# Routed outputs kept in DRAM until the last turn: stores and gathers in place of scatter matmuls

## What is computed

```python
ff = moe_swiglu(h, router_w[j], router_b[j], moe_w_gate[j], moe_w_up[j], moe_w_down[j])
x = x + g2 * ff
```

## Time and profile before

| What | Value |
|---|---|
| Median of 3 runs | 2793.11 us |
| Lowest and highest run | 2789.71 and 2797.35 us |
| The profiled execution | 2798.93 us |
| Its span, first to last instruction | 2797.2 us |
| Mean granted clock of TensorE | 0.992 |
| Busy, TensorE / VectorE / ScalarE / GpSimd | 2730.0 / 2003.7 / 1674.6 / 34.0 us |
| Read from and written to HBM | 695.19 and 8.91 MB |

### The profile page before, as it was taken

One profiled execution on the slowest core, in us unless ns is written; L12 is line 12 of the kernel. 1 busy time (PEld: TensorE's weight loads), 2 busy tenths in 40 slices (PEclk: granted clock), 3 DMA queues, 4 the chain that ended last, 5 costly groups with the idle time before them and its releaser, 6 DMA issues. The chain is left out here.

```text
span 2797.2 us, 39251 instructions
## 1 busy us (share of the span) xinstructions
PE 2730.0 (98%) x15544; PEld 2306.2 (82%) x15544; DVE 2003.7 (72%) x2123; ACT 1674.6 (60%) x1983; POOL 34.0 (1%) x60
## 2 busy tenths in 40 slices
PE   7999999999999999999999999999999999999998
PEld 5888999788978888888888888888868898867897
DVE  3766645586779989999898998986565556474555
ACT  3575544568457777777777777775354445353544
POOL 0000000000010000000000000001000000000000
PEclk8999999999999999999999999999999999999999
DMA  9847653765589999999999999975423453514451
GB/s 339 299 151 256 252 194 135 269 230 189 167 293 373 360 372 365 373 363 363 371 365 371 364 368 362 366 268 183 150 99 137 175 207 134 180 61 151 172 197 76
DMA packets 314443, 706.04 MB, mean 252 GB/s; under 512 B 7622, under 2 KB 26548, under 8 KB 314308
## 3 DMA queue, kind: packets, MB, share of 16 engines
q1 hardware_dynamic: 310336, 693.79, 69.0%
q0 software_dynamic: 3360, 10.16, 1.1%
q10 hardware_dynamic: 612, 0.18, 0.0%
HBM read 695.19 MB, written 8.91 MB: 252 GB/s over the span
## 5 line engine op out<-in xcount | busy, mean ns | idle before, releaser
L2731 DVE TENSOR_TENSOR ring_rest<-ring,weights_hi 128x2048 fp32r<-128x2048 f32 x270 | 608.3, 2283 | 10.1 <-ACT weights_hi L2056 8.1
L2056 ACT ACTIVATE weights_hi<-ring 128x2048 fp32r<-128x2048 f32 x270 | 516.6, 1915 | 134.7 <-PE ps L1782 71.6
L1780 PE MATMUL ps<-weights_hi,xg_hi 128*128 128x512 f32 x1008 | 402.4, 399 | 1.2 <-ACT arena L2056 0.6
L1782 PE MATMUL ps<-weights_hi,xg_lo 128*128 128x512 f32 x1008 | 395.1, 392 | 0.0
L1781 PE MATMUL ps<-ring_rest,xg_hi 128*128 128x512 f32 x792 | 309.9, 391 | 0.0
L2056 ACT ACTIVATE arena<-ps 128x512 f32<-128x512 f32 (+6 forms) x307 | 157.5, 529 | 220.5 <-PE ps L1782 54.1
L1801 PE MATMUL ps<-weights_hi,hidden_split_moe 128*128 128x512 f32 x1008 | 283.6, 393 | 0.1
L2731 DVE TENSOR_TENSOR ring_rest<-ring,mix_hi 128x2048 fp32r<-128x2048 f32 (+2 forms) x76 | 171.0, 2254 | 128.9 <-ACT mix_hi L2056 128.2
L2731 DVE TENSOR_TENSOR w_split<-ring,w_split 128x1024 fp32r<-128x1024 f32 x128 | 150.8, 1221 | 151.3 <-ACT w_split L2056 151.3
L2731 DVE TENSOR_TENSOR late_rest<-arena,weights_hi 128x2048 fp32r<-128x2048 f32 x108 | 245.3, 2285 | 5.5 <-ACT weights_hi L2056 4.5
L2056 ACT ACTIVATE weights_hi<-arena 128x2048 fp32r<-128x2048 f32 x108 | 207.1, 1918 | 65.9 <-PE ps L1782 36.0
(11 more groups left out here) (313 smaller groups left out, 5332.3 us busy)
## 6 DMA issues: line engine op xcount, KB each, us to landing
ring<-in_moe_w_gate_dram SPq DMA_DIRECT2D x54, 2048.0 KB, 8.5
ring<-in_moe_w_up_dram SPq DMA_DIRECT2D x45, 2048.0 KB, 9.2
ring<-in_moe_w_down_dram SPq DMA_DIRECT2D x36, 2048.0 KB, 8.2
ring<-in_mlp_w_dram SPq DMA_DIRECT2D x32, 2048.0 KB, 8.6
arena<-in_moe_w_down_dram SPq DMA_DIRECT2D x27, 2048.0 KB, 8.0
ring<-in_w_mod_dram SPq DMA_DIRECT2D x48, 1024.0 KB, 9.1
ring<-in_w_in_dram SPq DMA_DIRECT2D x48, 1024.0 KB, 6.1
arena<-in_moe_w_up_dram SPq DMA_DIRECT2D x18, 2048.0 KB, 8.0
```

The lines of the kernel that those rows point to most:

```text
L1780: pe.matmul(b, xg_hi[:, k, :], hi[:, i, :], start=(k == 0), stop=False)
L1782: mm = pe.matmul(b, xg_lo[:, k, :], hi[:, i, :], start=False, stop=(k == KD - 1))
L2056: return act.activation(o, i, func, **kw)
L2731: return dve.tensor_tensor(o, a, b, op)
```

## The change

A second DRAM table `y_rows` of the same shape as `slot_rows` is also filled with zeros, by eleven more writes. The event "scatter" goes, with its matmuls, its banks, its adds into x, and the rounding and splitting of the outputs in all turns but the last. In each turn but the first, SP stores `y_slots` (the outputs of the turn before) to that turn's 128 rows of `y_rows`, before the load of the twelfth of the 21 weights; SP has then waited for the first down product of this turn. VectorE waits for that store before it writes `y_slots` again. The first turn doesn't gate outputs that don't exist. When all turns are over (skipped ones count themselves), POOL gathers the rows of `y_rows` by `row_index` into `xn_moe`: two plain indirect DMAs for the first index of each token, a wait for them, and two accumulating ones for the second. VectorE adds the two tiles (128 x 1024) to x ahead of the last scatter, which stays. `weighted` moves to the place of `y_hi`, since `y_slots` now lives longer.

```diff
@@ expert_events, Tiles.expert_part
-        if what == "up" and half and g < 2:
-            events.append(("scatter", g))
-            elif kind == "scatter":
-                for t in range(TT):
-                    self.add(("scatter", e, at[0], t), "dve")
@@ program
-        slot_rows = nc.dram_tensor("slot_rows", (TURNS * P, D), F32).ap()
+        slot_rows, y_rows = (nc.dram_tensor(name, (TURNS * P, D), F32).ap() for name in ("slot_rows", "y_rows"))
+
+        def rows_of_turn(table, e):
+            return table.rearrange("(e p) d -> e p d", p=P)[bass.ds(e, 1)].rearrange("e p d -> p (e d)")
-        weighted = Region(y_at, TT * P).cut(TT, P)
         y_hi_at = expert.pos
+        weighted = Region(y_hi_at, TT * P).cut(TT, P)
@@ sync, load_turn; at its end in skipped turns, and once before the first turn
+                        if i == RING_B + expert_slots().index(("down", 0)):
+                            sp.dma_start(rows_of_turn(y_rows, turn - 1), y_slots).then_inc(sem("y_stored"), 16)
...
+                sp.sem_inc(sem("y_stored"), 16)
+
+            sp.sem_inc(sem("y_stored"), 16)
@@ gpsimd
                     for e in range(TURNS):
                         load(slot_rows[e * P:(e + 1) * P, :], blank, "slot_rows_blank")
+                        load(y_rows[e * P:(e + 1) * P, :], blank, "slot_rows_blank")
...
+            pool.wait_ge(sem("y_stored"), 16 * TURNS)
+            for n in range(2 * TT):
+                if n == TT:
+                    pool.wait_ge(sem("y_back"), 16 * TT)
+                pool.indirect_dma_start(xn_moe[:, n % TT], None, y_rows,
+                                        bass.IndirectOffsetOnAxis(row_index[:, n:n + 1], 0),
+                                        compute_op=ALU.bypass if n < TT else ALU.add).then_inc(sem("y_back"), 16)
 
             pool.wait_ge(pe_done, value["moe_down", TURNS - 1, GROUPS - 1])
             load(mem_nat, I["mem_2"][0].rearrange("(t p) d -> p t d", p=P), "mem_landed")
@@ tensor, expert_part
-                    elif kind == "scatter":
-                        c = at[0]
-                        if c == 0:
-                            pe.wait_ge(sem("to_tokens_hot_ready"), 1 + e)
-                        pe.wait_ge(sem("y_split_ready"), (c + 1) + e * 2)
-                        for t in range(TT):
-                            scatter(open_at(lambda i: ("scatter", i, c, t), e), t, c, y_hi[:, :])
@@ scalar, expert_head and expert_turn
-                    elif kind == "scatter":
-                        if at[0] == 0:
-                            act.wait_ge(pe_done, step_at(lambda i: ("scatter", i, 0, TT - 1), e))
-                            round_y(1, y_hi[:, :], e)
-                round_y(0, y_hi[:, :], e)
@@ vector
-            def first_half_of_y(e):
-
-                rest_of_y(0, y_hi[:, :], e)
+            def outputs_taken(e):
+
+                dve.wait_ge(sem("y_gated"), 2 * e)
                 dve.sem_inc(acc_emptied, 1)
...
-                        if (what, g, half) == ("gate", 1, 0):
-                            rest_of_y(1, y_hi[:, :], e)
-                    elif kind == "scatter":
-                        c = at[0]
-                        for t in range(TT):
-                            dve.wait_ge(pe_done, step_at(lambda n: ("scatter", n, c, t), e))
-                            xs = x[:, t, c * 512:(c + 1) * 512]
-                            tt(xs, xs, bank(("scatter", 0, c, t)), ALU.add).then_inc(emptied["dve"], 1)
@@ vector, expert_turn
+                dve.wait_ge(sem("y_stored"), e * 16)
                 gated_y(step_at(lambda i: ("moe_down", i, GROUPS - 1), e, 1))
                 rest_of_weights_of(4, e)
-                first_half_of_y(e)
+                outputs_taken(e)
@@ vector, first turn
+            dve.sem_inc(acc_emptied, 1)
             rest_of_routing()
-            gated_y(step_at(lambda i: ("moe_down", i, GROUPS - 1), 0, 1))
             rest_of_weights_of(4, 0)
-            first_half_of_y(0)
@@ vector, behind the last turn
+            def add_stored():
+
+                dve.wait_ge(sem("y_back"), 16 * 2 * TT)
+                for t in range(TT):
+                    tt(x[:, t], x[:, t], xn_moe[:, t], ALU.add).then_inc(sem("y_added"), 1)
+
+            dve.wait_ge(sem("y_stored"), 16 * TURNS)
             gated_y(value["moe_down", TURNS - 1, GROUPS - 1])
             for c in range(2):
-                rest_of_y(c, last_y_hi[:, c], TURNS)
+                rest_of_y(c, last_y_hi[:, c])
             dve.sem_inc(acc_emptied, 1)
+            add_stored()
+            dve.wait_ge(sem("y_added"), TT)
             for t in range(TT):
                 for c in range(2):
                     b = full(dve, ("last_scatter", 2 * t + c))
```

More of the change, by code:

```diff
@@ L735, in program @@
         expert.cut(HI_BUFFERS * 2048 + HALF_LINE)
-        y_hi, y_lo = rounded("y_hi", y_hi_at, 512), rounded("y_lo", y_at, 2, 512)
+        y_lo = rounded("y_lo", y_at, 2, 512)
         last_y_hi = rounded("last_y_hi", route_at, 2, 512)
@@ L1114, in load_turn @@
                             sp.wait_ge(sem("rows_scattered"), 16 * 2 * TT)
-                            rows_of_turn = slot_rows.rearrange("(e p) d -> e p d", p=P)[bass.ds(turn, 1)]
-                            sp.dma_start(rows_moe, rows_of_turn.rearrange("e p d -> p (e d)"))\
+                            sp.dma_start(rows_moe, rows_of_turn(slot_rows, turn))\
                                 .then_inc(sem("slot_rows_landed"), 16)
+                        if i == RING_B + expert_slots().index(("down", 0)):
+                            sp.dma_start(rows_of_turn(y_rows, turn - 1), y_slots).then_inc(sem("y_stored"), 16)
                     elif stream.before[n]:
@@ L1200, in _ @@
                                pattern=[[1, P]], channel_multiplier=-1).then_inc(sem("route_constants"), 1)
-            pool.wait_ge(sem("slot_rows_blank"), 16 * TURNS)
+            pool.wait_ge(sem("slot_rows_blank"), 32 * TURNS)
             pool.wait_ge(sem("row_index_ready"), 1)
@@ L1869, in _ @@
                 if i < 2:
-                    pe.wait_ge(sem("y_split_ready"), 2 * TURNS + i + 1)
+                    pe.wait_ge(sem("y_split_ready"), i + 1)
                 scatter(open_bank(("last_scatter", i)), i // 2, i % 2, last_y_hi[:, i % 2])
@@ L2339, in _ @@
                 if l:
-                    act.wait_ge(sem("slot_rows_blank"), 16 * TURNS)
+                    act.wait_ge(sem("slot_rows_blank"), 32 * TURNS)
                 gelu(0)
@@ L2452, in _, with round_y @@
             scale, shift = modc[:, 1, 3 * KD:4 * KD], modc[:, 1, 2 * KD:3 * KD]
-            def round_y(c, dst, e):
-                act.wait_ge(sem("y_gated"), (c + 1) + e * 2)
+            def round_y(c, dst):
+                act.wait_ge(sem("y_gated"), 2 * (TURNS - 1) + c + 1)
                 f(dst, y_slots[:, c * 512:(c + 1) * 512], ACT.Copy).then_inc(sem("y_rounded"), 1)
@@ L2539, in skipped @@
                 act.sem_inc(sem("to_tokens_ready"), 1)
-                act.sem_inc(sem("y_rounded"), 2)
             taken[0] += 1
@@ L2551, in _ @@
                 round_weights_of(p, 0)
-            round_y(0, y_hi[:, :], 0)
             round_weights_of(5, 0)
@@ L2561, in _ @@
             for c in range(2):
-                round_y(c, last_y_hi[:, c], TURNS)
+                round_y(c, last_y_hi[:, c])
             f(st[:, 2 * TT + 2:2 * TT + 3], eps, ACT.Sqrt)
@@ L3302, in gated_y, with rest_of_y @@
                         gb[:, 1, c * 512:(c + 1) * 512], ALU.mult, ALU.mult).then_inc(sem("y_gated"), 1)
-            def rest_of_y(c, rounded_part, e):
-                dve.wait_ge(sem("y_rounded"), (c + 1) + e * 2)
+            def rest_of_y(c, rounded_part):
+                dve.wait_ge(sem("y_rounded"), c + 1)
                 tt(y_lo[:, c], y_slots[:, c * 512:(c + 1) * 512], rounded_part.bitcast(F32), ALU.subtract)\
@@ L3398, in skipped @@
                 dve.sem_inc(sem("to_tokens_hot_ready"), 1)
-                for name in ("y_gated", "y_split_ready"):
-                    dve.sem_inc(sem(name), 2)
+                dve.sem_inc(sem("y_gated"), 2)
             taken[0] += 1
```

## The result

| | before | after |
|---|---|---|
| median of 5 runs, us | 2793.29 | 2777.64 |
| lowest to highest, us | 2789.71 to 2801.55 | 2775.66 to 2780.79 |
| profiled execution, us (span) | 2798.9 (2797.2) | 2779.5 (2777.7) |

The ratio is 0.993, with a 95% interval from 0.9901 to 0.996, that is 11 to 28 us. The change is worth 15.65 us between the medians; 2779.4 us was forecast.

A forecast was written before the change was run, and what follows sets the result against it. TensorE was taken to set the turns' pace, DMA engines close behind. -14.7 - 3.5 + 2.3 + 1.7 + 0.5 = -13.7 us took the profiled 2798.9 to 2785.2, 5.8 above the median scale: 2779.4 us; range 2770 to near 2795.

The forecast's parts named there:

- Part 1: In the turns: scatter matmuls leave TensorE's stream, 1.84 us a turn over eight turns, -14.7 us.
- Part 2: First turn, bound by VectorE: its shorter chain brings the first down projection from 832.0 to 828.5, -3.5 us.
- Part 3: One 512 KB store in each turn: costs nothing if the DMA engines manage 377 GB/s.
- Part 4: Feed-forward part: eleven more 512 KB blank writes delay the second `ffn_up` load to 344.3 us; 0, bound 3 us.
- Part 5: After the turns: four gathers done at 1896, hidden with 12 us to spare; two new adds are not hidden.
- The adds: Before the last scatter's first add: two 128x1024 adds of 1.23 us each on the chain, +2.3 us.
- The clock at the end: Near the turning of x: TensorE stands some 2.8 us, one more stretch of lower clock follows, +1.7 us.
- The load beside the gathers: End of the turns: the second gather pair may share the DMA engines with a load on the chain, +0.5 us.
- The DMA ceiling: Rival, in the turns: DMA engines sustain only 366 GB/s, a turn takes 123.2 us, kernel 2808 us; chance 0.08.
- The unrealised gain: Rival, in the turns: VectorE's chains hold TensorE, only first turn and end count, kernel 2794 us; chance 0.05.
- The late gathers: Rival, after the turns: gathers land late, +18 us at the end, kernel 2797 us; chance 0.07.

The follow-up runs named there:

- The third blank: The changed kernel with the blank written a third time, into a table that nobody reads: 2779.17 us, ratio 0.9959 to the kernel before.
- the four spare stores: The changed kernel storing each turn's outputs five times over, 2.1 MB a turn more: 2782.31 us, ratio 0.9949 to the kernel before.

## Why the prediction was right

- **Part 1, the matmuls in the turns: -14.7, measured -14.70** over eight turns in the profile, with 119.65 to 119.70 us from one turn to the next. That TensorE's work made it is shown by the kernel that put the eight matmuls back (121.46 us, nothing left of the gain in the turns) and the one that put VectorE's back (119.65 us).
- **Part 2, the first turn: -3.5, measured -4.01.** The term named the first down product at 828.5; it came at 828.80, from a start 0.8 us later. The chain was the one worked out. That it was VectorE's is shown from both sides: TensorE's matmuls put back 0.0 us, part of VectorE's work put back 1.8 up to that down product and 1.6 behind it, and 4.5 us of routing taken off it brought 4.5 more. What left the chain there (gating, two `y_lo`, two adds) is 3.7 us in the timeline of the kernel before, close to the 4.01; no run put all of it back.
- **Part 3, the store: 0, measured 0**, with 378 GB/s against the 377 worked out. The cover was put at 3 us a turn, from 387 GB/s. This was too small: 394 GB/s go without a wait in the turns.
- **Part 4, the blank: 0, measured 0**, and the narrowest of the margins. The landing was forecast at 344.3 us and came at 345.15: the issue was 1.5 us later, and the landing took 29.3 us instead of 16.1 + 13.8. The reading was taken wrongly. The rounding at 344.73 is that of `ffn_gate`; `ffn_up` is read 1 us later, so the margin was forecast at 0.4 us and was 1.4 by the same rows. Measured it is 1.1 us. The third blank, 4.8 us more, shows that there is hardly more room than that.
- **Part 5, the gathers: hidden, as forecast.** The way from the first issue to the last landing was put at 26 us and took 16.2. A pair needed 7.0 and 9.0 us rather than 13. So there were 20 us to spare and not 12. The adds: +2.3, measured +2.08.
- **The clock at the end: +1.7, measured 0.** This term was wrong. It rested on TensorE standing 2.8 us ahead of the turning of x. The row shows 0.76 us. The forty dummy matmuls of `keep_busy` are released by VectorE's add behind the two new ones, so they moved along: they begin 3.65 us behind the last scatter's first matmul and not 2.04. In one profiled execution of the changed kernel the clock did fall twice around there, under the scatter and behind the first mixing matmul, in the other not at all, and the way from the last scatter to the mixing was 13.42 us in both.
- **The load beside the gathers: +0.5, measured +1.06, but for another reason.** The load took 9.99 us instead of 8.95, yet the gathers had landed before it was issued. In the kernel with the matmuls put back, which has the same gathers, it took 9.0 us. It took 10.0 to 10.2 in each of the kernels with a turn of 119.7 us where nothing fell beside it. What couples the two stays open.

Summed up: the gains (turns and first turn) were put at 18.2 us and came to 18.7; the costs were put at 4.5 and came to 3.1. That is the 1.8 us by which it ended below the forecast. The mechanism of the gain was right; part of the closeness is luck. The clock's term was 1.7 too high and the load's 0.6 too low, and the medians of two groups (15.65 and 17.4) differ by as much as the miss.

**The rivals.** The DMA ceiling is excluded as far as 394 GB/s, by the four spare stores. The unrealised gain is excluded by the length of the turns and by the kernel with VectorE's work put back. The late gathers were not there; when they were held back, their mechanism cost 7.7 us.

## What to carry to other kernels

Two resources at 100% of a turn aren't both the bound: the one without a single wait is (TensorE here), and the other, share 1.00, took 2 MB more in each turn without effect on the turns. A rate read from a trace in which nobody waits for a load is a floor for what the DMA engines can do and not a ceiling. Where one row of a timeline joins two operations, look which of them reads the tile in question before working out a margin from its start. Price an early stage separately from the steady one, even if it runs the same code: what bounds the first turn (VectorE, just come from the routing) isn't what bounds the eight after it, and here moving 4.5 us of small operations out of that chain shortened the first turn by 4.5 us, beside the 15.65 that the whole change brought.

## What the runs showed that I had not expected

- The DMA engines sustained 394 GB/s of reads and stores mixed, over whole turns, with landings of 15.1 us instead of 9.9.
- An accumulating gather of a 512 KB tile took 6.4 and 7.1 us to land, a plain one 4.4 and 5.7, without other transfers; beside the weight loads all four were at 9.7 in the median.
- A load's landing can differ by 1 us (8.95 and 9.0 against 10.0 to 10.2) between kernels in which nothing else is under way. Unexplained.
- Falls of the granted clock to its lower level come and go between executions of the same kernel (1.00 and 0.61 at one place), and move its time by some us.
